# Per-token factors spread by a transpose of a widened row instead of by a product

## The reference

```python
e = jnp.exp(logits - m)                                  # attention, all branches
den = jnp.sum(e, axis=-1, keepdims=True)                 # one sum per token and head
p = (e / den).astype(vb.dtype)
...
y = xf * lax.rsqrt(jnp.mean(xf * xf, axis=-1, keepdims=True) + NORM_EPS)   # norms, one factor per token
```

## Time and profile before

| | |
|---|---|
| median of 3 runs | 3492.5 us (3491.12 to 3495.15) |
| the profiled execution | 3497.21 us, span 3495.4 us |
| TensorE busy | 3382.3 us (97%), 20142 matmul records |
| weight loads busy | 2803.2 us (80%) |
| VectorE busy | 2067.7 us (59%), 3295 instructions |
| ScalarE busy | 1370.2 us (39%) |
| GpSimd busy | 189.2 us (5%) |
| mean granted TensorE clock | 0.989 |

### The profile page before, as it was taken

The page is one execution under the profiler, slowest core; times in us unless marked ns, Lnnn a source line. Parts: engine busy times, 40 slices in busy tenths (PEclk is TensorE's granted clock), DMA queues, the critical chain, the costliest instruction groups (busy, mean ns, idle before and its releaser), DMA issues.

```text
span 3495.4 us, 53703 instructions
## 1 busy us (share of the span) xinstructions
PE 3382.3 (97%) x20142; PEld 2803.2 (80%) x20142; DVE 2067.7 (59%) x3295; ACT 1370.2 (39%) x2167; POOL 189.2 (5%) x45
## 2 busy tenths in 40 slices
PE   8999999999999999999998999999999979999998
PEld 7766888888877678888888777988888878788887
DVE  7876557444688745645566554653544665556546
ACT  6556333222463643322213554341322336534323
POOL 2311000000133010000000000000000000000000
PEclk9999999999999999999999999999999989999999
DMA  4245232222223633322221001121121220112222
GB/s 143 85 157 204 101 118 109 96 96 96 84 97 106 234 120 109 128 96 96 97 96 49 13 13 57 49 72 61 61 72 50 72 73 13 57 61 108 96 96 85
DMA packets 45783, 317.15 MB, mean 91 GB/s; under 512 B 5008, under 2 KB 7312, under 8 KB 8464
## 3 DMA queue, kind: packets, MB, share of 16 engines
q1 hardware_dynamic: 44720, 307.07, 24.6%
q10 hardware_dynamic: 864, 7.31, 0.5%
HBM read 312.26 MB, written 2.10 MB: 90 GB/s over the span
## 4 chain that ended last, share of the span: by engine, by line
PE 83%; DVE 9%; ACT 4%; issue 2%; DVEq 2%; DMA 1%; POOL 0%; SPq 0%; ACTq 0%; POOLq 0%
PE psum L801 22%; PE psum L802 21%; PE psum L805 21%; PE psum L1456 3%; PE psum L1490 2%; PE psum L1474 2%; DVE MA L2449 2%; PE psum L1287 1%; ACT whi L1673 1%; PE psum L885 1%; PE psum L948 1%; DVE BQK L2213 1%; PE psum L1420 1%; PE psum L1279 1%; PE psum L1280 1%
## 5 line engine op out<-in xcount | busy, mean ns | idle before, releaser
L801 PE MATMUL psum<-xh,whi 128*128 128x512 f32 (+1 forms) x2224 | 854.6, 386 | 2.7 <-issue 1.6
L802 PE MATMUL psum<-xl,whi 128*128 128x512 f32 (+1 forms) x2224 | 848.6, 384 | 0.0
L1673 ACT ACTIVATE whi<-wst 128x2048 fp32r<-128x2048 f32 x233 | 445.0, 1910 | 558.6 <-PE psum L805 537.6
L2195 DVE TENSOR_TENSOR wlo<-wst,whi 128x2048 fp32r<-128x2048 f32 x199 | 455.9, 2291 | 175.0 <-ACT whi L1673 173.3
L805 PE MATMUL psum<-xh,wlo 128*128 128x512 f32 (+1 forms) x2224 | 536.4, 383 | 0.1
L801 PEld LDWEIGHTS psum<-xh,whi 128*128 128x128 f32 x2224 | 418.7, 188 | 94.6 <-issue 13.7
L802 PEld LDWEIGHTS psum<-xl,whi 128*128 128x128 f32 x2224 | 418.6, 188 | 81.4 <-issue 1.0
L805 PEld LDWEIGHTS psum<-xh,wlo 128*128 128x128 f32 x2224 | 409.8, 188 | 82.2 <-POOL wlo L763 0.5
L763 POOL TENSOR_TENSOR wlo<-wst,whi 128x2048 fp32r<-128x2048 f32 x40 | 188.4, 4711 | 2841.3 <-ACT whi L2053 1757.0
L801 PE MATMUL psum<-gh,whi 128*128 128x512 f32 (+1 forms) x576 | 186.0, 340 | 1.0 <-DVE gl L3106 1.0
L801 PE MATMUL psum<-uh,whi 128*128 128x512 f32 x480 | 186.9, 389 | 0.0
(11 more groups left out here) (399 smaller groups left out, 5801.0 us busy)
## 6 DMA issues: line engine op xcount, KB each, us to landing
wst<-weights SPq DMA_DIRECT2D x287, 1024.0 KB, 4.8
dft<-c_dft ACTq DMA_DIRECT2D x2, 2688.0 KB, 10.7
hT<-x_t SPq DMA_DIRECT2D x4, 512.0 KB, 8.3
wst<-weights SPq DMA_DIRECT2D x2, 512.0 KB, 5.9
cT<-ctx_t ACTq DMA_DIRECT2D x1, 1024.0 KB, 7.3
out<-hT SPq DMA_DIRECT2D x1, 1024.0 KB, 4.9
out<-hT SPq DMA_DIRECT2D x2, 512.0 KB, 3.4
masks<-c_masks SPq DMA_DIRECT2D x1, 644.0 KB, 11.4
```

The costliest lines, as they stand in the source:

```text
L801: pe.matmul(out, weights(m.whi, k), head(k), start=opens and n == 0, stop=False)
L802: pe.matmul(out, weights(m.whi, k), tail(k), start=False, stop=False)
L1673: act.activation(m.whi[:, slot, :], m.wst[:, slot, :], ACT.Copy).then_inc(s.hi_ready, 1)
L2195: TT(m.wlo[:, slot, :], m.wst[:, slot, :], m.whi[:, slot, :].bitcast(F32), ALU.subtract).then_inc(s.lo_ready, 1)
```

## The change

The stationary operand is turned with `pe.transpose` instead of multiplied with the identity. For the norm factors it stays the column repeated with stride zero. In the attentions the two products of a unit (one per head, 64 columns each) become one transpose of 128 columns; for this VectorE writes a row of 128 values first, 64 times the one factor and 64 times the other, into a new tile (`inv`, `inv2`, two buffers each). A drain stands between the reciprocal and the copy, and the semaphore is raised by the copy.

```diff
@@ denominators(l, u), first attention, TensorE
-                for par in range(2):
-                    c = 2 * (u % 4) + par
-                    last = pe.matmul(ps[6][HD * par:HD * (par + 1), P:2 * P], m.rden[:, c:c + 1].broadcast_to([P, HD]),
-                                     ident, start=True, stop=True)
-                last.then_inc(s.rs_done, 1)
+                pe.transpose(ps[6][:, P:2 * P], m.inv[:, u % 2, :], ident).then_inc(s.rs_done, 1)
@@ spread2(name), norms
-                    last = pe.matmul(ps[4 + number % 4][:, b * P:(b + 1) * P],
-                                     m.roots[:, number % 4, b:b + 1].broadcast_to([P, P]), ident, start=True, stop=True)
+                    last = pe.transpose(ps[4 + number % 4][:, b * P:(b + 1) * P],
+                                        m.roots[:, number % 4, b:b + 1].broadcast_to([P, P]), ident)
@@ the combined norm at the start of the second stack
-                                        last = pe.matmul(ps[bank][:, b * P:(b + 1) * P], factor.broadcast_to([P, P]), ident,
-                                                         start=True, stop=True)
+                                        last = pe.transpose(ps[bank][:, b * P:(b + 1) * P], factor.broadcast_to([P, P]), ident)
@@ denominators(u), second attention, TensorE
-                    for par in range(2):
-                        c = 2 * (u % 4) + par
-                        last = pe.matmul(ps[bank][VH * par:VH * (par + 1), 0:P],
-                                         m.rden2[:, c:c + 1].broadcast_to([P, VH]), ident, start=True, stop=True)
-                    last.then_inc(s.t2_done, 1)
+                    pe.transpose(ps[bank][:, 0:P], m.inv2[:, u % 2, :], ident).then_inc(s.t2_done, 1)
@@ reciprocals(l, u), first attention, VectorE
-                nc.vector.reciprocal(m.rden[:, 2 * (u % 4):2 * (u % 4) + 2], m.den[:, 2 * (u % 4):2 * (u % 4) + 2]
-                                     ).then_inc(s.rden_ready, 1)
+                c = 2 * (u % 4)
+                nc.vector.reciprocal(m.rden[:, c:c + 2], m.den[:, c:c + 2])
+                dve.drain()
+                nc.vector.tensor_copy(m.inv[:, u % 2, :].rearrange("p (a d) -> p a d", a=2),
+                                      m.rden[:, c:c + 2].unsqueeze(2).broadcast_to([P, 2, HD])).then_inc(s.rden_ready, 1)
@@ reciprocals(u), second attention, VectorE
-                    nc.vector.reciprocal(m.rden2[:, c:c + 2], m.den2[:, c:c + 2]).then_inc(s.rden2_ready, 1)
+                    nc.vector.reciprocal(m.rden2[:, c:c + 2], m.den2[:, c:c + 2])
+                    dve.drain()
+                    nc.vector.tensor_copy(m.inv2[:, u % 2, :].rearrange("p (a d) -> p a d", a=2),
+                                          m.rden2[:, c:c + 2].unsqueeze(2).broadcast_to([P, 2, VH])).then_inc(s.rden2_ready, 1)
```

More of the change, by code:

```diff
@@ L478, in two_stacks @@
         m.warm, at = place(nc, at, "warm", [P, 1])
+        m.inv, at = place(nc, at, "inv", [P, 2, P])
         assert at <= 229376, at
@@ L564, in two_stacks @@
         ko0, _ = place(nc, ko0_area, "ko0", [P, TA])
+        m.inv2, at_ = place(nc, ko0_area + 4 * TA, "inv2", [P, 2, P])
+        assert at_ <= v_area + 8 * KT * TC
         m.Ko = ko0, ko1
```

## The result

The changed kernel takes 3520.2 us (median of 4 runs, 3519.0 to 3523.5) against 3491.9 beside it: a ratio of 1.0079, 95% interval 1.0067 to 1.0091, that is 28 us slower. The forecast was 3500.3, with a range of 3485 to 3508. The sign was right, the size and the range were wrong.

The account below looks back on a forecast made before the run. The prediction took TensorE as the main bound, 83% of the span on the chain. Its terms, 3.2 + 5.3 - 5.1 + 3.1 + 1.7 + 2.2 - 2.6 = +7.8 us, took the median 3492.5 to 3500.3, range 3485 to 3508.

Parts of the forecast that it names:

- VectorE, one unit: Added drain and 128-element copy in each attention unit: 0.31 us, with ends 0.25 and 0.67.
- the sum: All priced steps on the chain, in both attentions and the norm factors: +7.8 us; chance 0.46.
- 5.3 + 3.1 + 1.7 + 2.2: VectorE's added us: first attention 5.3; second attention's turns 3.1 in layer 1, 1.7 in layer 0; its turned-group copy 2.2.
- 17 C units with a selection: First attention: the chain passes through the reciprocal 17 times, each paying 0.31 us, +5.3 us.
- the eight turns of layer 1: Second attention, where no projection lies between: turns go from 1.23 to 1.5 us, 10 units paying 0.31, 3.1 us.
- 3.2 - 5.1: TensorE's spreads: first attention 36 units 0.09 us dearer, +3.2; second attention 46 units 0.11 cheaper, -5.1.
- Norms: 50 norm-factor products become transposes; 24 on the chain save 0.11 us each, -2.6 us, ends -1 and -5.8.
- Dearer VectorE: Rival: each of the second attention's 48 latent units, not 17, pays 0.31 us; sum +17.9, 3510.4 us; chance 0.09.
- Two records: Rival: a turned row with stride zero takes two records as a product does; +19.5, 3512 us; chance 0.02.
- Cover: Rival: the second attention's +7.0 us of delays folds into existing waits; +0.8, 3493.3 us; chance 0.27.
- not slower: Rival: turned row costs no shape change, copy mostly falls into VectorE's waits; -8.9, 3483.6 us; chance 0.13.
- The clock: Rival: TensorE falls to the lower clock once more in each of four stages, +8 us, 3508 us; chance 0.03.

Follow-up runs that it names:

- before_short_gpsimd: Kernel before the change, with GpSimd's subtractions cut from 2048 to 16 columns: 3488.4 us, 5.9 us faster than the kernel before as it is.
- reduce_widens: Changed kernel with the widening copy written as a maximum over an axis of length one: 3504.7 us against 3493.8 for the kernel before, ratio 1.0032.
- the pair with the short subtraction: Changed kernel and kernel before, both with GpSimd's subtractions cut to 16 of 2048 columns: 3495.4 against 3488.4 us, difference 7.1.
- vector_only: Kernel before plus only VectorE's added drain and widening copy in both attentions, all spreads still products: 3526.1 us against 3493.4, ratio 1.0094, +32.6 us.
- tensor_only: Kernel before with one transpose of the identity replacing the two products in both attentions, VectorE and norms unchanged: 3491.9 us against 3493.4, ratio 0.9994.
- the two ScalarE kernels: Changed kernel with ScalarE widening the row, in both attentions (3494.8 us) or with the first attention as before (3492.8), against 3493.8 for the kernel before.
- reciprocal_twice: Changed kernel with the widening copy replaced by a reciprocal of the wide-read sums, same drain and instruction count: 3559.7 us, ratio 1.0187 to the kernel before.

## Why the prediction was wrong, by its own steps

**VectorE, one unit: the step that failed.** I priced drain and copy at 0.31 us by the cast of the earlier trace rows and bounded that by 0.25 and 0.67. Undisturbed the price was right: from the reciprocal to the instruction behind the copy 0.30 more passes than before, in both attentions (0.55 for 0.25, and 0.37 for 0.08). But a price for one undisturbed instruction was taken for all 132, and nine of them stood beside GpSimd: the sum put that wait at nothing and gave no reason. The part alone measured +32.6 where the sum has 5.3 + 3.1 + 1.7 + 2.2 = 12.3. The kernel before had shown the behaviour in a line that I did not read, of VectorE's two-input operation on tiles in SBUF in the stage ahead of the first attention:

```profile
L2449 DVE SCALAR_TENSOR_TENSOR MA<-R,IW,MA x48: 483/620/4650, 102.9 to 1085.2; 128x256 f32<-128x256 f32 x16, 128x384 f32<-128x384 f32 x16, 128x512 f32<-128x512 f32 x16
```

A maximum of 4.65 beside a median of 0.62 and a GpSimd instruction of 4.6 is the signature. Eight of these 48 start inside a subtraction and take 4.3 to 4.7; no other takes over 0.76. That GpSimd is the cause is shown by before_short_gpsimd, where the long ones are gone:

```profile
L2449 DVE SCALAR_TENSOR_TENSOR MA<-R,IW,MA x48: 483/619/753, 100.3 to 1075.3; 128x256 f32<-128x256 f32 x16, 128x384 f32<-128x384 f32 x16, 128x512 f32<-128x512 f32 x16
```

Laying the reciprocals of before over GpSimd's records, as the two fences at 2913 do, finds the places. The nine copies were held for 24.7 us; what that cost is 17 (28.3 less the 10.9 of reduce_widens) to 21 us (less the 7.1 of the pair with the short subtraction), the lower clock behind them included. With it my 3500.3 becomes 3517 to 3521, which tests the plain part of the sum only: the price of the held copies is measured and not forecast.

The Trainium skill ("SBUF — State Buffer", Who interferes with whom) has the rule: VectorE's second pair of SBUF ports is GpSimd's only one; a copy, a cast or a `tensor_scalar` from SBUF to SBUF may take both pairs, a reduction on this chip never does, and whoever comes second waits for the whole instruction. By that rule the copy was the wrong kind for this place. The traces agree: copies end within 0.1 us of GpSimd's 4.55, reductions of 0.286 and copies out of PSUM of 0.67 run beside it. The rule also says that a two-input instruction with both inputs in SBUF is blocked while GpSimd reads; the two lines of L2449 agree.

**VectorE's plain time was right.** In the 17 C units with a selection I had 5.3 us; vector_only is 2.4 + 2.4 us longer over the C units of the two layers. In the second attention the eight turns of layer 1 were to take 1.5 us; from 3032.77 to 3034.31 they take 1.54. For the whole of it I had 7.0; reduce_widens less tensor_only gives 4.6 + 4.3 = 8.9, with a record of 0.286. Without long copies the whole change measures +10.9 (reduce_widens; 7 to 15 by its interval) or +7.1 (the pair), and the sum said +7.8.

**TensorE.** The sum had 3.2 - 5.1 = -1.9; measured -1.6. Its pieces, from the chain after, first a B unit, then the end of a unit of the last stage and the products behind it:

```profile
269.98 0.59 PE psum L928 x8
270.56 0.26 PE psum L937
270.82 0.65 PE psum L855 x8
```

```profile
2997.59 1.46 PE psum L1488 x24
2999.05 0.26 PE psum L1498
2999.31 0.30 PE psum L1418
2999.61 0.23 PE psum L1419
```

The transpose with the change of shape ahead of it takes 0.26, not the 0.31 that I added up. In the first attention that is +0.04 against the 0.22 of the earlier trace rows; tensor_only grows by 0.30 us over 12 such units, 0.025 each, where I had 0.09. In the second attention 0.26 + 0.07 (0.30 less 0.23, for the product behind) = 0.33 stands against 0.22 + 0.20 of the earlier trace rows: 0.09 saved, where I had 0.11. It holds for all 60 units, not for the 46 that I counted: tensor_only is 3.3 us shorter there, and would be 1.3 to 1.7 more without the fall of the clock (an estimate from the step at that fall), where I had 5.1. The direction of both was right, each a little smaller.

**Norms.** -2.4 against -2.6, inside the noise.

**The rivals.** "Dearer VectorE" named the right engine and the wrong form: it had 0.31 in each of 48 units; the chip paid nothing beyond my count in most and about 4 in a few. "Two records" fell by the 72 and 60 single records. "Cover" and "not slower" had nothing held either. "The clock" expected falls from the transposes themselves. In the changed kernel the extra falls of the last stage stand behind the waits for the long copies, where the products of the values take 0.7 to 1.3 us more; in tensor_only and the two ScalarE kernels one fall costs 1.3 to 1.7 us. My range ended at 3508 because its high side rested on a dearer copy everywhere, at 1 in 30, and had no case in which one engine stops another. (Its high end for VectorE adds up to 27.0, not 26.6; nothing hangs on that.)

## What to carry to other kernels

Before a plain SBUF-to-SBUF copy goes onto VectorE, lay its places over GpSimd's records. Where they meet, the copy lasts until GpSimd's instruction ends, and that counts if something that TensorE waits for stands behind it in VectorE's queue. The wait stands inside the copy's own duration, not in idle time, so a group's maximum against its median (4.40 against 0.227) tells it at once, and its mean (0.41) does not. A stall of 3 us on TensorE may cost more than its length, since the granted clock can be lower behind it. If the two meet, give the copy to ScalarE where it has room, write it as a reduction, or cut GpSimd's instruction into pieces.

## What was not expected of the hardware

A reciprocal of 128x128 takes 0.953 us, four times a copy (0.227), while one of 128x2 takes 0.16. A maximum over an axis of one takes 0.286. GpSimd's subtraction of 2048 columns takes 4.55 in one piece and 5.58 in eight. Of the time that the long reciprocal adds over the reduction (132 x 0.667 = 88 us), 55 us reached the end (65.5 over before, less 10.9): VectorE's queue had less room in the attentions than its 59% of busy time suggests (some of it is the clock: its mean is 0.983 in reciprocal_twice, 0.989 before).
